# Second-chunk-onward up projections of four convolution FFN stages in 128-token halves instead of 256-token products

## What is computed

```
def conv_glu_ffn(h, up_w, conv_w, conv_b, down_w):
    gate, up = jnp.split(h @ up_w, 2, axis=-1)
    gate = causal_dwconv(gate, conv_w) + conv_b
    return (jax.nn.silu(gate) * up) @ down_w
...
x = x + conv_glu_ffn(rmsnorm_2(x, ln_ffn[i]), f_up[i], f_conv_w[i], f_conv_b[i], f_down[i])
```

## Time and profile before

| | before |
|---|---|
| median of 3 runs | 4009.58 us (3997.74 to 4010.38) |
| the profiled execution's own time | 4006.53 us |
| its span | 4004.8 us |
| TensorE busy | 3823.6 us (95%) |
| VectorE, ScalarE busy | 1061.4 us (27%), 721.6 us (18%) |
| DMA | 149 GB/s mean |

### The profile page before, as it was taken

The page is one execution under the profiler, slowest core; times in us unless marked ns, Lnnn a source line. Parts: engine busy times, 40 slices in busy tenths (PEclk is TensorE's granted clock), DMA queues, the critical chain, the costliest instruction groups (busy, mean ns, idle before and its releaser), DMA issues.

```text
span 4004.8 us, 37903 instructions
## 1 busy us (share of the span) xinstructions
PE 3823.6 (95%) x16756; PEld 2747.2 (69%) x16756; DVE 1061.4 (27%) x2069; ACT 721.6 (18%) x1361; POOL 16.4 (0%) x43
## 2 busy tenths in 40 slices
PE   6999999999999999999995899999999999999998
PEld 5856785875587775778564568667666877757684
DVE  5434341502410243112103202126420212431120
ACT  1004200001510242111001111023221102521110
POOL 1000000000000000000000000000000000000000
PEclk9999999999999999999996899999899999999999
DMA  9752584744234423334440124332222434333342
GB/s 374 283 199 107 212 300 176 276 147 147 107 145 154 153 106 126 131 130 160 147 147 21 65 105 168 141 135 103 106 107 105 153 142 154 119 121 132 132 154 88
DMA packets 42451, 598.45 MB, mean 149 GB/s; under 512 B 4736, under 2 KB 4752, under 8 KB 6192
## 3 DMA queue, kind: packets, MB, share of 16 engines
q1 hardware_dynamic: 41024, 589.94, 40.0%
q0 software_dynamic: 1264, 6.10, 0.4%
HBM read 594.97 MB, written 1.05 MB: 149 GB/s over the span
## 4 chain that ended last, share of the span: by engine, by line
PE 92%; DVE 5%; ACT 2%; issue 1%; DMA 0%; DVEq 0%
PE ps L449 33%; PE ps L328 12%; PE ps L345 9%; PE ps L1906 4%; PE ps L2202 3%; PE ps L361 3%; PE ps L2221 3%; PE ps L1939 2%; PE ps L1414 2%; PE ps L1064 1%; PE ps L1409 1%; PE ps L1434 1%; PE ps L474 1%; PE ps L645 1%; PE ps L371 1%
## 5 line engine op out<-in xcount | busy, mean ns | idle before, releaser
L449 PE MATMUL ps<-hT,ring 128*128 128x256 f32 (+1 forms) x7360 | 1327.7, 343 | 3.6 <-DVE stat L309 3.6
L449 PEld LDWEIGHTS ps<-hT,ring 128*128 128x128 f32 x7360 | 1194.9, 191 | 134.2 <-issue 7.7
L328 PE MATMUL ps<-ring,aT 128*128 128x512 f32 x1088 | 477.4, 600 | 20.1 <-DVE aT L2326 14.5
L328 PEld LDWEIGHTS ps<-ring,aT 128*128 128x128 f32 x1088 | 208.2, 193 | 280.2 <-issue 257.3
L345 PE MATMUL ps<-ring,aT 128*128 128x512 f32 x848 | 371.1, 595 | 9.0 <-ACT aT L2266 7.8
L345 PEld LDWEIGHTS ps<-ring,aT 128*128 128x128 f32 x848 | 160.1, 191 | 205.4 <-issue 194.4
L208 DVE SCALAR_TENSOR_TENSOR memT<-big,silu_c,memT 128x512 f32<-128x512 f32 x238 | 179.0, 752 | 8.5
L1906 PE MATMUL ps<-hT,ring 128*128 128x256 f32 x768 | 173.1, 382 | 0.0
L383 ACT ACTIVATE big<-x 128x1024 f32<-128x1024 f32 x34 | 35.9, 1057 | 759.5 <-DVE x L426 432.5
L1906 PEld LDWEIGHTS ps<-hT,ring 128*128 128x128 f32 x768 | 145.5, 191 | 26.1 <-issue 7.7
L426 DVE TENSOR_TENSOR x<-x,ps 128x1024 f32<-128x1024 f32 x22 | 26.9, 1221 | 432.1 <-PE ps L345 432.1
(11 more groups left out here) (481 smaller groups left out, 3450.0 us busy)
## 6 DMA issues: line engine op xcount, KB each, us to landing
ring<-weights_in SPq DMA_DIRECT2D x244, 2048.0 KB, 7.7
big<-ada_in SPq DMA_DIRECT2D x34, 2048.0 KB, 7.7
ring<-ada_in SPq DMA_DIRECT2D x2, 2048.0 KB, 27.4
big<-b_gate_in POOLq DMA_DIRECT2D x1, 1536.0 KB, 15.1
x<-x_in SPq DMA_DIRECT2D x1, 1024.0 KB, 5.0
big<-b_gate_in POOLq DMA_DIRECT2D x1, 1024.0 KB, 9.0
big<-mem_in POOLq DMA_DIRECT2D x1, 1024.0 KB, 5.3
out<-big SPq DMA_DIRECT2D x2, 512.0 KB, 2.6
```

What stands on the lines that cost most here:

```text
L328: last = pe.matmul(ps[:, 2 * t + half, :], aT[:, 4 * j + k, t * P:(t + 1) * P], w[:, k, half * 512:(half + 1) * 512], start=(4 * j + k == ...
L449: last = pe.matmul(ps[:, bank + m // 2, (m % 2) * SEQ + at:(m % 2) * SEQ + at + n], w[:, k, m * P:(m + 1) * P], hT[:, k, at:at + n], start ...
```

## The change

In the nine later chunks of each of the four convolution stages, the call on 256 tokens becomes two calls, first on tokens 0 to 127 and then on tokens 128 to 255. The semaphore of the chunk is raised after the last product of the second half. Nothing else is changed: the same banks, the same columns of them, and the same waits.

```diff
@@ convglu_pe @@
                 pe.wait_ge(convglu_dve_done, 44 * n + 4 * j - 4)
                 w = arrived(pe, c0 + j).rearrange("p (k c) -> p k c", k=KT)
-                channels_pe(pe, w, 4 + 2 * (j % 2)).then_inc(chunks_used, 1)
+                for t in range(TT):
+                    last = channels_pe(pe, w, 4 + 2 * (j % 2), t)
+                last.then_inc(chunks_used, 1)
```

## The result

| | before | after |
|---|---|---|
| median | 4004.96 us (3995.78 to 4010.38, 5 runs) | 4026.01 us (4024.49 to 4028.03, 5 runs) |
| the profiled execution | 4006.53 us | 4024.49 us |
| its span | 4004.8 us | 4022.8 us |

The kernel is slower: the ratio of the times is 1.0056, with a 95% interval of 1.0038 to 1.0074. The medians differ by 21.05 us and the two profiled executions by 18.0 us.

What follows compares the result with a forecast made beforehand. TensorE was taken to bound the kernel. Only the matmuls' 17.2 us counted: on the profiled 4006.5 us it gives 4023.7, with the median 3.1 us higher 4026.8; forecast 4025 us, range 4013 to 4035.

Steps and rivals of the forecast that it cites:

- What bounds the kernel: In the convolution stages' L449 pieces TensorE has no gaps, so any change in distance between record starts goes into the total.
- The two prices: In the nine later chunks, 215.87 ns a wide record, 111.67 a narrow one: 7.47 ns more per pair, 17.2 us in all.
- What the narrow price is made of: A 128-token record in the convolution stages: two passes of 53.33 ns with 5.0 ns on top instead of 2.5.
- The step on the weight loads: In the convolution chunks each half reloads all 32 tiles, overlapping the matmuls and already in the measured starts; nothing added.
- The first rival: Narrow price belongs to the first chunks; long stretches run at 109.1 ns a record: 5.2 us more, 4015 us; chance 7%.
- The second rival: Instruction supply in the convolution stages: 18 added blocks become bare time, 17.5 us on top, 4044 us; chance 4%.
- The third rival: Granted clock drops inside the long convolution stretches, another 1.7 us at each stage: 4032 us; chance 4%.
- The clock behind the stages' ends: Slow clock at the down projections' start, up to 1.7 us at each of four ends: taken as 0, range ±6.8 us.
- every other piece of the chain keeps its length: Sign expected in the profile after: outside the four L449 pieces, which grow to 150.1 us, no piece of the chain changes.

Runs made afterwards that it cites:

- the late wait: Kernel before, wide products; down projection starts once the chunk before the last is multiplied, awaiting the last only ahead of tiles reading it: 3971.87 us, ratio 0.9893.
- the early gate: Kernel before, wide products; TensorE raises a semaphore when a chunk's gate half is done and ScalarE starts on that: 3979.13 us, ratio 0.9924.
- the halves on top of it: The early gate plus the change's halves, gate tiles in both halves and then up tiles in both: 3995.93 us, ratio 0.997 to the kernel before.

## Why the prediction was right, point by point

**What bounds the kernel** was right. The pieces of L449 had no slack, and all that was added in them came out in the total.

**The two prices** were right as prices, and the sum with them. 215.87 and 111.67 ns gave 7.47 ns a pair, 4.3 us a stage and 17.2 us in all; the four pieces show 4 x 4.31 = 17.2. The median of 4026.0 is 1 us beyond the forecast, and that it is so near is in part luck. The forecast stood on a base of 4006.5 or 4009.6 us; over five runs the median of before is 4004.96, and 17.2 us on top of that would be 4022.2.

**What the narrow price is made of** was wrong, without harm to the sum. I read it as "two passes of 53.33 ns, has 5.0 ns on top instead of 2.5", an overhead of the matmul. The runs show a floor set by the weight load. It is 111.65 ns for 64 tokens as well and 109.3 ns for 128 tokens with half the load, so 128 tokens are bound by their load, just below the point where the two lengths meet. The step on the weight loads was therefore wrong in its words too: "The loads overlap the matmuls in both forms" hides that the load is off the path at 256 tokens (215.87 ns with a full load and 216.1 with half of it), while at 128 tokens it is what sets the pace. The loads were costed at nothing rightly only because the measured distance contained them. The fixed 2.5 ns of the Trainium skill, "TensorE: Matmul & The Clock Gate", section "Back-to-back issue gap", fits 136, 160, 192 and 256 tokens here, and 128 and 64 tokens when the load is shorter (109.3 ns, and 55.9 with 32 loaded columns). It does not fit where the load is the longer of the two. The prediction left out that the same section limits its formula: in a stream of weight loads and matmuls both set the spacing, and at small widths the formula comes out too low because it has no term for the load. The trace agrees with that (111.67 ns against the formula's 109.2).

**The first rival**, a price of the neighbourhood with a floor of 109.1 ns, is excluded: 1152 narrow records in a row cost the same 111.67 ns each, in all four stages. Its floor was a misread row; the true one is 111.6 ns, and with it the rival would have had no price of its own.

**The second rival**, the supply of instructions, did not show. There is no gap in any piece, with 18 more blocks, and none in the stretch with 58.4 ns a record, which uses instructions 1.9 times as fast as the change.

**The third rival**, a slower clock in the stage, did not occur in the change: 1.00 throughout. The worry had ground, though. With 32 tokens a record and full loads the clock fell to 0.50 and stayed.

**The clock behind the stages' ends** was taken as 0 with both ends kept. The first three down projections took 1.3, 1.2 and 0.7 us more than before and the last 0.2 us less, 3.1 us together. Other stages took 2.3 us less on balance, since the spans differ by 18.0 and not by 20.3. So "every other piece of the chain keeps its length" did not hold to the letter, and the total came within 1 us of the four pieces because two small misses cancel in part (+3.1 and -2.3 us).

**What else moves the time.** In the runs further up, layers that nobody edited differed by more than that. The largest such difference lies between the second and the third convolution stage, in the layer with the gated delta mixer. The chain in order of time shows the first products of that layer and those of the third convolution stage, before:

```profile
2654.87 7.23 PE ps L449 x64
...
3116.05 7.14 PE ps L449 x64
```

And with the late wait:

```profile
2638.23 7.22 PE ps L453 x64
...
3087.82 7.14 PE ps L453 x64
```

From one start to the other that is 461.18 us before and 449.59 with the late wait: 11.6 of the 15 us that the ends do not explain. By stretches, the 50 us that begin 270 us after the start of the second stage's down projection, before and with the late wait:

```profile
2838.48:2888.48 50.00, 47.09 (x403) 32.45 (x403) 7.76 (x8) 8.31 (x12) 0.00 (x0) 0.77 0.25 90
```

```profile
2823.80:2873.80 50.00, 47.13 (x505) 33.59 (x504) 13.04 (x15) 11.03 (x16) 0.00 (x0) 1.00 0.26 96
```

The granted clock is 0.77 in the one and 1.00 in the other. My estimate of what that costs is (1.00 - 0.77) x 50 = 11.5 us, which is the size of the difference. In the early gate the same distance is 464.77 us, with 0.77 in the same stretch, and with the halves on top of it 451.08 us. So this layer alone can shift a time by more than 10 us, in kernels whose edits lie elsewhere. That it also makes the spread of before (3995 to 4019 us in these sessions) and the rest of the early gate's median is likely but not shown, since only one execution of each has a trace. Why the clock falls there in one execution and not in another stays open.

## What to carry to other kernels

Price a split by the distance between starts in a gapless stretch of the same form, not by the mean length of a record or by a short group cut at its edges. In f32 with full weight tiles a product with 128 tokens runs at the pace of its weight load, and more splitting costs a whole load each: 4 x 64 tokens took 257.24 us where 256 took 124.34. Look at the ends of such stages before their inside: moving one wait behind work that does not need it gained 26.9 us at the four ends, where the halves lost 17.2. And compare stage by stage: the medians of that pair differ by 42 us, of which 15 lie in layers that nobody edited, as its two traces show.

## What the runs showed of the hardware that I had not expected

- A weight load costs 5.0 ns over its columns and a matmul 2.5 ns, and a record costs the longer of the two (with the output partitions varied along with the load): 111.65, 85.0 and 58.4 ns for 128, 96 and 64 loaded columns with 64 tokens, but 109.3 and 109.2 ns for 64 and 96 loaded columns with 128 tokens.
- Loading the tile that was just loaded has no discount (111.67 ns).
- TensorE can be busy in every record and still lose its clock: at 32 tokens a record with full loads the granted clock was 0.50 for some 485 us, and a record took 213.5 ns there.
